# Starting the first layer by groups of 512 channels while its modulation is still being computed

## The reference, cut to what matters

```python
mod = jnp.dot(jax.nn.silu(c), w_ada) + b_ada          # c: 2048, w_ada: 2048 x 6144
shift, scale, gate = jnp.split(mod, 3, axis=-1)
u = rms_norm(x, norm_w) * (1.0 + scale[:, None, :]) + shift[:, None, :]
proj = jnp.dot(u, w_in)                               # w_in: 2048 x 19064
```

## Time and profile before

| | |
|---|---|
| Median of three runs | 3601.93 us (3600.55 to 3607.24) |
| The profiled execution | 3606.82 us, span 3605.0 us |
| TensorE busy | 3485.0 us, 97% |
| VectorE, ScalarE, GpSimd busy | 2280.1, 1689.4, 31.1 us |
| Read from memory | 696.45 MB, 195 GB/s over the span |
| Mean granted TensorE clock | 0.977 |

### The profile page before, as it was taken

One profiled execution on the slowest core, in us unless ns is written; L12 is line 12 of the kernel. 1 busy time (PEld: TensorE's weight loads), 2 busy tenths in 40 slices (PEclk: granted clock), 3 DMA queues, 4 the chain that ended last, 5 costly groups with the idle time before them and its releaser, 6 DMA issues. The chain is left out here.

```text
span 3605.0 us, 45068 instructions
## 1 busy us (share of the span) xinstructions
PE 3485.0 (97%) x18836; PEld 2997.6 (83%) x18836; DVE 2280.1 (63%) x2722; ACT 1689.4 (47%) x2076; POOL 31.1 (1%) x61
## 2 busy tenths in 40 slices
PE   7999999998999999999999999999999999999998
PEld 7779878877888887799888888888888789988887
DVE  7687666756677456677655576664566676554544
ACT  2354564454333344545644543433445775443333
POOL 0000000000000000000000000000000000000000
PEclk7899999999999999999999999999999999999999
DMA  9654455456667545444444367765555444455554
GB/s 374 231 203 158 152 199 198 175 185 231 257 253 287 200 181 196 163 161 146 162 144 149 124 223 254 256 258 193 187 187 181 167 166 141 153 211 193 191 186 153
DMA packets 99387, 705.67 MB, mean 196 GB/s; under 512 B 11680, under 2 KB 11696, under 8 KB 15600
## 3 DMA queue, kind: packets, MB, share of 16 engines
q1 hardware_dynamic: 93888, 675.38, 51.5%
q0 software_dynamic: 4864, 24.95, 2.0%
q10 hardware_dynamic: 432, 2.45, 0.2%
HBM read 696.45 MB, written 6.29 MB: 195 GB/s over the span
## 5 line engine op out<-in xcount | busy, mean ns | idle before, releaser
L1365 ACT ACTIVATE HH<-RAW 128x2048 fp32r<-128x2048 f32 x546 | 1045.2, 1914 | 1201.5 <-PE G L1107 905.1
L1701 DVE TENSOR_TENSOR LL<-RAW,HH 128x2048 fp32r<-128x2048 f32 x546 | 1248.0, 2287 | 337.2 <-ACT HH L1365 335.8
L1107 PE MATMUL G<-HH,UH 128*128 128x512 f32 x2560 | 1028.0, 402 | 33.2 <-DVE LL L1701 27.6
L1107 PE MATMUL G<-LL,UH 128*128 128x512 f32 x2560 | 1006.4, 393 | 0.0
L1107 PE MATMUL G<-HH,UL 128*128 128x512 f32 x2560 | 1006.0, 393 | 0.0
L1107 PE MATMUL G<-UH,HH 128*128 128x256 f32 x2080 | 605.0, 291 | 14.5 <-DVE LL L1701 8.4
L1107 PEld LDWEIGHTS G<-HH,UH 128*128 128x128 f32 x2560 | 485.9, 190 | 154.2 <-DVE LL L1701 37.4
L1107 PE MATMUL G<-UL,HH 128*128 128x256 f32 x2080 | 590.5, 284 | 0.0
L1107 PE MATMUL G<-UH,LL 128*128 128x256 f32 x2080 | 590.4, 284 | 0.0
L1107 PEld LDWEIGHTS G<-LL,UH 128*128 128x128 f32 x2560 | 485.6, 190 | 104.9
L1107 PEld LDWEIGHTS G<-HH,UL 128*128 128x128 f32 x2560 | 486.4, 190 | 102.2 <-issue 4.1
(11 more groups left out here) (327 smaller groups left out, 2506.9 us busy)
## 6 DMA issues: line engine op xcount, KB each, us to landing
RAW<-in_w_in_packed_dram SPq DMA_DIRECT2D x402, 1024.0 KB, 4.8
RAW<-in_w_ada_packed_dram SPq DMA_DIRECT2D x96, 1024.0 KB, 5.1
RAW<-in_w_out_packed_dram SPq DMA_DIRECT2D x48, 1024.0 KB, 4.8
RAW<-in_w_o_ssd_packed_dram SPq DMA_DIRECT2D x32, 1024.0 KB, 4.8
RAW<-in_w_o_fox_packed_dram SPq DMA_DIRECT2D x16, 1024.0 KB, 4.8
RAW<-in_w_o_dsa_packed_dram SPq DMA_DIRECT2D x16, 1024.0 KB, 5.2
RAW<-in_w_proj_a_packed_dram SPq DMA_DIRECT2D x16, 1024.0 KB, 4.8
RAW<-in_w_proj_b_packed_dram SPq DMA_DIRECT2D x16, 1024.0 KB, 4.8
```

Of the source, the lines that this page charges most:

```text
L1107: mm = pe.matmul(to, lt, rh, start=first, stop=end, skip_group_check=True)
L1365: a.activation(HH[g % NH][:, :n], RAW[ch["f"] % NR][:, :n], ACT.Copy).then_inc(*hi_done.up(g))
L1701: v.tensor_tensor(LL[f % NR][:, :n], RAW[f % NR][:, :n], HH[g % NH][:, :n].bitcast(F32), ALU.subtract).then_inc(*lo_done.up(g))
```

## The change

**Groups.** The modulation chunks come in the order shift block g, scale block g, for g = 0 to 3. When both are folded, `am` and `u` are made for the 512 channels of group g. `open` writes this part of the plan: in the windows of groups 1, 2 and 3, between the eight modulation chunks, stand three weight chunks, those of `iq` 0, `iq` 1 and `dk` for the channels of the group before. The last chunks of these three blocks follow after group 3 in the usual way. `dk` gets a third bank set, made of `BA` and `BC`; `misc` comes after `dk`.

**Modulation in the opening.** VectorE keeps one accumulator. For every fourth chunk ScalarE writes four products (`PROD`) and GpSimd adds them up. TensorE only folds, into `BD` or `BE`. In the diff, `ada` with `gp` is GpSimd's part and `ada_prod_a` ScalarE's.

**Buffers.** Four more `RAW` and `LL` buffers lie where `YH` and `YL` stand later; the opening uses nine.

**x.** Both squares come first; then ScalarE scales the first x tile and VectorE the second. Two turned pieces of x come in each slot instead of one. Layer 1's modulation (`every` = 2 of 5) now starts after the three blocks.

```diff
-NR, NH = 5, 3
+NR, NX, NH = 5, 4, 3
...
+        buf = self.next_buf % (NR + NX if self.opening else NR)
...
+    def open(self, blocks, ready, enter):
+        behind = None
+        for gi in range(4):
+            todo = [("ada",)] * 8
+            if gi:
+                for i, b in zip((2, 5, 8), blocks):
+                    todo.insert(i, ("w", b["chunks"][gi - 1]))
+            for kind, *ch in todo:
+                if kind == "ada":
+                    self.ada_fetch()
+                    self.ada_chunk()
+                    if behind:
+                        self.gemm(behind)
+                        behind = None
+                else:
+                    behind = ch[0]
+                    behind["g"] = len(self.chunks)
+                    self.chunks.append(behind)
+                    behind["f"] = self.fetch(behind["src"], ("gemm_done", behind["g"]))
+                    self.put("hi", behind["g"])
+                    self.put("lo", behind["g"])
+                self.slot()
+            if behind:
+                self.gemm(behind)
+                behind = None
+            self.until(self.ada["job"])
+            self.until(ready)
+            enter(gi)
+        self.ada["both"], self.opening = False, False
+        self.next_buf = 0
+        for b in blocks:
+            self.push(b["chunks"][3])
...
     def first_x():
         for t in range(2):
+            put("x_square", t)
+        for t in range(2):
             put("x_norm", t)
-            yield
+        yield
         for c in range(KT // 2):
             put("x_in", c)
-            yield
+            if c % 2:
+                yield
...
+    def enter_first(gi):
+        put("am", 0, gi)
+        put("u", 0, gi)
+        ended("u_lo", 0, 2 * gi + 1)
...
-    o.ada["list"] = [(0, b, k) for b in range(8) for k in range(4)]
+    o.ada["list"] = [(0, b, k) for gi in range(4) for b in (gi, 4 + gi) for k in range(4)]
     put("start")
-    for gen in (first_x(), load_layer(0), rope(0), rope(1)):
+    came = o.side.add(first_x())
+    for gen in (load_layer(0), rope(0), rope(1)):
         o.side.add(gen)
-
-    o.ada_all()
-    while o.side.q:
-        o.slot()
-    o.ada["both"] = False
-    o.ada["list"] += [(1, b, k) for b in range(8) for k in range(4)]
-    o.evac.add(modulated(0))
-    entered = [o.evac.add(enter(0, gi)) for gi in range(4)]
+    entered = []
...
+        first = ((IQ, ("iq", l, 0)), (IQ + 512, ("iq", l, 1)), (DK, ("dk", l, 0)))
+        if l == 0:
+            fb = [o.wblock(w, c0, heads(h), u_ready, kind="tm", begun=True, which=i) for i, (c0, h) in enumerate(first)]
+            o.open(fb, came, enter_first)
+            o.ada["list"] += [(1, b, k) for b in range(8) for k in range(4)]
...
     GB = [[bank("G0"), bank("G1")], [bank("G2"), bank("G3")]]
     BA, BC, BD, BE = bank("BA"), bank("BC"), bank("BD"), bank("BE")
+    GB.append([BA, BC])
...
+        def ada(i):
+            gp.wait_ge(*ada_prod.at(i, 1))
+            gp.tensor_tensor(PROD[0], PROD[0], PROD[1], ALU.add).then_inc(*ada_gp.up(i, 0))
+            gp.wait_ge(*ada_prod.at(i, 3))
+            gp.tensor_tensor(PROD[2], PROD[2], PROD[3], ALU.add).then_inc(*ada_gp.up(i, 1))
+            gp.wait_ge(*ada_gp.at(i, 0))
+            gp.wait_ge(*ada_gp.at(i, 1))
+            gp.tensor_tensor(acc, PROD[0], PROD[2], ALU.add).then_inc(*ada_gp.up(i, 2))
...
+        def ada_prod_a(i):
+            for k in range(4):
+                a.activation(PROD[k], R[:, k * 512:(k + 1) * 512], ACT.Copy,
+                             scale=CT1[:, e["kc"] * 4 + k:e["kc"] * 4 + k + 1]).then_inc(*ada_prod.up(i, k))
```

More of the change, by code:

```diff
@@ L109, in __init__ @@
         self.packed = {}
+        self.opening, self.next_buf, self.buf_user = True, 0, {}
         self.fetches = []
@@ L195, in gemm @@
                 self.slot()
-            b["free"] = user["free_by"] or user["end"] if user is not None else ("start",)
+            if user is None:
+                b["free"] = ("x_put", KT // 2 - 1) if b["set"] == 2 else ("start",)
+            else:
+                b["free"] = user["free_by"] or user["end"]
         self.put("gemm", ch["g"], 0)
@@ L209, in gemm, with begin @@
                 b["after"](ch["g"])
-    def block(self, chunks, evac, x, ready, kts, needs=None, after=None, soon=None):
-        b = {"n": len(self.blocks), "set": len(self.blocks) % 2, "x": x, "ready": ready, "kts": kts, "evac": evac, "needs": needs or (lambda k0: []),
-             "after": after, "job": None, "free_by": None, "end": None}
+    def begin(self, chunks, evac, x, ready, kts, which=None, needs=None, after=None, soon=None):
+        if which is None:
+            which = self.turns % 2
+            self.turns += 1
+        b = {"n": len(self.blocks), "set": which, "x": x, "ready": ready, "kts": kts, "evac": evac, "chunks": chunks,
+             "needs": needs or (lambda k0: []), "after": after, "soon": soon, "job": None, "free_by": None, "end": None}
         self.blocks.append(b)
@@ L216, in block, with wblock @@
             ch.update(block=b, first=i == 0, end=i == len(chunks) - 1)
+        return b
+    def block(self, *args, **kw):
+        b = self.begin(*args, **kw)
+        for i, ch in enumerate(b["chunks"]):
             self.push(ch)
-            if i == 1 and soon:
-                self.until(soon()[0])
+            if i == 1 and b["soon"]:
+                self.until(b["soon"]()[0])
         return b
-    def wblock(self, w, c0, evac, ready, kind="cm", x=("U", 0), kts=KT, **kw):
+    def wblock(self, w, c0, evac, ready, kind="cm", x=("U", 0), kts=KT, begun=False, **kw):
         chunks = []
@@ L230, in wblock @@
             chunks.append({"src": src, "w": 512, "nk": 4, "k0": kc * 4, "parts": parts})
-        return self.block(chunks, evac, x, ready, kts, **kw)
+        return (self.begin if begun else self.block)(chunks, evac, x, ready, kts, **kw)
     def ada_fetch(self):
@@ L626, in work_order @@
                "w": 128, "nk": 16, "k0": 0, "parts": [("cm", 0, 0, 0, P, 0)]}
+        first = ((IQ, ("iq", l, 0)), (IQ + 512, ("iq", l, 1)), (DK, ("dk", l, 0)))
[3 more added lines that the diff above has]
+            o.ada["list"] += [(1, b, k) for b in range(8) for k in range(4)]
+        else:
+            fb = [o.wblock(w, c0, heads(h), u_ready, kind="tm", needs=None if i else u_needs,
+                           soon=None if i else (lambda e=entered: e)) for i, (c0, h) in enumerate(first)]
         o.ada["every"] = (2, 5) if l == 0 else 0
-        iq_b = [o.wblock(w, IQ, heads(("iq", l, 0)), u_ready, kind="tm", needs=u_needs, soon=(lambda e=entered: e))]
         misc_b = o.block([one], misc(l), ("U", 0), u_ready, KT)
-        iq_b.append(o.wblock(w, IQ + 512, heads(("iq", l, 1)), u_ready, kind="tm"))
         o.side.add(o.when([misc_b], misc_work(l)))
-        o.side.add(o.when(iq_b, index_scores(l)))
-        dkv_b = o.wblock(w, DK, heads(("dk", l, 0)), u_ready, kind="tm")
+        o.side.add(o.when(fb, index_scores(l)))
+        dkv_b = fb[2]
         dq_b = [o.wblock(w, DQ + j * 512, heads(("dq", l, j)), u_ready, kind="tm") for j in range(2)]
@@ L791, in hybrid_stack @@
         c.__exit__(None, None, None)
+    for tiles, dt in ((RAW, F32), (LL, F32R)):
+        over = []
+        for i in range(NR, NR + NX):
+            c = nc.sbuf_tensor(f"{'RAW' if tiles is RAW else 'LL'}{i}", [P, 2048], dt)
+            over.append(c)
+            tiles.append(c.__enter__())
+        for c in reversed(over):
+            c.__exit__(None, None, None)
     YH = sb("YH", [P, KT, S], F32R)
@@ L805, in hybrid_stack @@
     early = QQ[:, :, :].rearrange("p a b -> p (a b)")
+    PROD = [early[:, 2048 + k * 512:2048 + (k + 1) * 512] for k in range(4)]
     ACCS = [(early[:, 0:512], early[:, 512:1024]), (early[:, 1024:1536], early[:, 1536:2048])]
@@ L847, in hybrid_stack @@
     start = count("start", [()])
[L848 removed]
+    raw = [count(f"raw{i}", [(f,) for f, e in enumerate(o.fetches) if e["buf"] == i], 16) for i in range(NR + NX)]
     ld_c, ld_cst = count("ld_c", [()], 16), count("ld_cst", [()], 16)
@@ L1114, in begin @@
             pe.wait_ge(*ld_cst.at())
[L1116 to L1126, removed]
-                    mm = pe.matmul(bk[:, j:j + 1], R[:, k * 512 + j * P:k * 512 + (j + 1) * P], CT1[:, m0:m0 + 1],
-                                   start=k == 0 and j == 0, stop=False, skip_group_check=True)
-            mm.then_inc(*ada_pe.up(i))
         def fold_pe(n):
@@ L1142, in fold_pe @@
                 for m, acc in enumerate(accs):
-                    mm = pe.matmul(bk[:, j:j + 1], acc[:, j * P:(j + 1) * P], one1, start=m == 0 and not e["both"],
-                                   stop=m == len(accs) - 1, skip_group_check=e["both"])
+                    mm = pe.matmul(bk[:, j:j + 1], acc[:, j * P:(j + 1) * P], one1, start=m == 0,
+                                   stop=m == len(accs) - 1)
             mm.then_inc(*fold.up(n))
@@ L1148, in x_in @@
             bk = (BA, BC)[c % 2]
```

(3 more changed lines are left out.)

118 lines of the change are left out of this document (73 added, 45 removed).

## The result

The changed kernel takes 3656.9 us (median of 4 runs, 3651.5 to 3657.9) against 3601.3 us before: a ratio of 1.0148, 95% interval 1.013 to 1.0165, so it is slower by 1.5%. The forecast was 3598.8, in a range of 3587 to 3622. The profiled execution has a span of 3656.1 us, 51.1 more than before.

What follows compares the result with a forecast made beforehand. It took transfers to bound the opening and TensorE nearly everything else. Terms of -9.2, +3.1, +3.0 and 0 summed to -3.1 us, giving 3598.8 us from a median of 3601.9; range 3587 to 3622.

Steps and rivals of the forecast that it cites:

- the common point: Start of the first dq chunk: 194.0 before, forecast 184.8 after, a gain of 9.2 us.
- Four modulation tiles of layer 1 move from here to the merge stages: Tiles leaving the stretch of the dq blocks for the merge stages: same work in both places, so nothing.
- I take 1 us a group: Opening: cost to VectorE of GpSimd's adds, about one add's length for three, +3.0 us in all.
- -9.2 and +3.1: Gain up to the first dq chunk, and TensorE work done by then before that now comes later.
- First `fold_add` at 50: Opening: VectorE's squares, scaling, accumulations and rope stretches put the first group's fold_add at 50 us.
- Group of 34.2: Opening: one group's loop takes 34.2 us; t is when VectorE starts a group's second fold_add.
- The higher bound: Opening: three GpSimd adds charged in full to VectorE's critical stretch, a sum of +3.7 us instead of -3.1.
- From the last `fold_add` to the `dq` chunk, 32.2: End of opening: u and lo, three last chunks, iq turns and the misc chunk take 32.2 us.
- The `dq` stalls and the relief, nothing on balance: dq blocks: 3.4 us idle for misc copies against 3.4 regained from later index scoring; bounds -7 and +6.
- term (a): After the first dq chunk: turns, misc_pe and a fold formerly done by then come later, +3.1 us or nothing.
- GpSimd and VectorE exclude each other: Opening rival: adds wait until VectorE stands at fold_add; 41 us a group, +15 us, 3617; chance 0.13.
- the later schedule suffers: Rival: index scoring, attention and scan run five to nine chunks late; +10 us of idle, 3612; chance 0.09.

Runs made afterwards that it cites:

- a_vec: Changed kernel with first-merge-stage tiles at their old places, layer 1's misc between the iq blocks, and VectorE alone for the opening's modulation: 3612.9 us (1.0034).
- b_misc: Kernel before with the misc block behind dk in both layers instead of between the two iq blocks: 3629.4 us (1.0066).

## Why the prediction was wrong

The step that failed is the one after the common point: "Four modulation tiles of layer 1 move from here to the merge stages; the same work there as here, so nothing", and with it the whole reckoning to one common point, behind which both kernels were taken to run alike. The work was indeed the same (the stage takes 336.9 us with the four tiles and 337.2 without). But its places moved against blocks that did not, and in a stage that had next to no idle time (1.5 us of 337.2) this cost 20 to 26 us of the medians, shown from both sides. A second move was in the diff and not priced at all: `misc` behind `dk` in layer 1, 14 us there, also shown from both sides.

Ahead of these the opening failed as well, by the size of one term: "I take 1 us a group" for what GpSimd's adds cost VectorE. They cost it 5.4 us of its time and the group 3.8. With contention the first `dq` chunk was forecast near 188 and came at 202.9; of these 15.0 us 4.2 were there at the first `fold_add`, 8.6 came in the three groups, and 2.2 are a wait at the end. By the prediction's own sum, -9.2 and +3.1, the opening turns into a loss from 2.0 us a group on (it says 2.5).

Point by point, with the prediction's own terms:

- *First `fold_add` at 50*: 54.2. Both sets of adds ahead of it slowed VectorE: seven accumulations from 28.77 on took 8.19 us instead of 5.54, and two `rope` steps of 0.21 and 0.35 took 1.19 and 1.37. The terms as they are written, 37.2 + 11.4 + 2.5, give 51.1 and not 49.8.
- *Group of 34.2*: 38.0. TensorE's start was forecast at t + 11.6 and came at t + 14.3 (68.50 - 54.21); in a_vec, without GpSimd, it came at t + 11.7. The first chunk took 7.7 for a forecast of 7.9, fold A 1.84 for 1.85. The third chunk waited 1.2 to 1.4 us for its `lo`, forecast at nothing, since that `lo` ended at t + 30.6 instead of t + 25.0. (On VectorE's way there the text counts four accumulations; the plan, and the sum to 25.0, have three.) So the loop was right, and the term for GpSimd too small: 1 us a group, and worth 3.8. The higher bound that stood beside the Trainium skill's rule (GPSIMD Engine Reference, Specifications: interfaces shared with VectorE, contention when VectorE has two SBUF inputs) was the better choice. The trace agrees with that rule, 0.75 against 1.57 to 1.66 us an accumulation. The same line of the Trainium skill's page names a second case, VectorE instructions in a 2-port perf mode. `TENSOR_SCALAR`, with one large input, took 1.53 instead of 0.48 at 73.59, which would fit it; no row here shows in which mode it ran. The Trainium skill, Perfetto Trace Analysis, Optimizing Scalar/DVE Operations, warns that moving work between these two engines might not help; here it gave 0.6 us of 6.1.
- *From the last `fold_add` to the `dq` chunk, 32.2*: the turn ahead of it ended at 200.67, 32.25 behind 168.42. Right. But the chunk itself waited 2.2 us more for a copy on ScalarE.
- *The `dq` stalls and the relief, nothing on balance*: from chunk 13 (by its first product) to chunk 104 (by its `lo`) the difference went from +8.9 to +9.1 in the profiled execution, and to +20 in others of the same order. Without the 3.1 of term (a), which was owed in this stretch, that is -3 to +8, where the bounds were -7 and +6. How much of it is the idle time of the `dq` blocks was not separated.
- *The rivals*. That GpSimd and VectorE exclude each other (41 us a group) was 3 us too much, about as far off as the forecast (3.8 below, or 2.8 with its 1 us of contention). Its picture was half right: an accumulation that starts during an add is held up, but the adds are not put off until VectorE stops; both engines go on, slower. That the later schedule suffers was right in kind and got 9 in 100 and 10 us: b_misc lost 11 us ahead of chunk 104 by it. What it left out is that the same move stands in layer 1, with 14 us more. No rival held that the places in the merge stage would shift.

In the account of the kernel before, 34 tiles in 92.6 us are 2.7 us each, not 2.6; nothing turned on it.

What stays open is how the 9 to 20 us ahead of chunk 104 divide between the opening and the later index scoring. b_misc alone gives 11, and the opening alone put `dq` off by 8.9; they don't simply add, and a_vec, whose opening was 4 us shorter, had lost this again by chunk 92.

## What to carry to other kernels

When the order of work is planned by counters and lists, a change at the front moves everything that is spaced by them. Print both plans and compare them to the end: the differing lines at chunks 104 to 107 and 203 to 219 were there to be read before any run. What to look for is a wait that closes a loop, here a tanh that stands for a free bank, behind a `hi` that waits for TensorE's last product: TensorE cannot run ahead of either. Look, too, for two steps in one slot that need different tables on ScalarE. And work handed to GpSimd beside a VectorE that never rests need not be taken off VectorE: price it by what VectorE loses.

## What the runs showed of the hardware

An add 512 wide on GpSimd took 1.26 us with VectorE in short steps and 1.39 to 2.12 beside its accumulations. An accumulation on VectorE that started during such an add took 1.57 to 1.66 us instead of 0.75, one that had started before the add kept its 0.75 (59.68, with the add at 60.12), and ScalarE's products beside it changed nothing. So VectorE lost 2.6 us to three adds in one stretch (8.14 - 5.54) and 5.4 to the six of a group, where the work that they took off it was 6.1. A change of ScalarE's table took 1.28 us; the window of layer 1 had 30 of them with the scan three chunks late and 26 before. Around one wait of 5.1 us in a stretch of full work TensorE's granted clock was 0.75 (896 to 902) and then 0.53 (902 to 906), and around three of four waits of 2.67 us 0.78 to 0.84 for 6 us; around the fourth, at 917, it stayed at 1.00.
